# Feed-forward networks from seven products: a new order of splits, root and spread, and weight sums made by DMA

## The reference

```
def rms_norm(x, g):
    y = x * rsqrt(mean(x * x, axis=-1) + 1e-6)
    return y * g
def swiglu(h, w_gate, w_up, w_down):          # 1024 -> 2816 -> 1024
    return (silu(h @ w_gate) * (h @ w_up)) @ w_down
h = h + 0.5 * swiglu(rms_norm(h, gain), w_gate, w_up, w_down)
```

## Time and profile before

| | |
|---|---|
| median of 3 runs | 2536.75 us (2528.5 to 2537.78) |
| the profiled execution's own time | 2528.84 us |
| its span, first to last instruction | 2526.6 us |
| TensorE busy | 2434.3 us, 96% |
| VectorE busy | 1708.9 us, 68% |
| ScalarE busy | 1078.2 us, 43% |
| GpSimd busy | 97.3 us, 4% |
| mean granted TensorE clock | 0.986 of full speed |
| DMA | 213.00 MB, 84 GB/s; SP's queue takes 25.7% of the 16 engines' time |

### The profile page before, as it was taken

How to read it: one execution, slowest core, us unless ns; L and a number is a source line. 1 busy time by engine, 2 the same in 40 slices (tenths; PEclk the granted TensorE clock), 3 DMA queues, 4 the chain that set the end, 5 groups by cost and what they waited for, 6 DMA issues and landing times.

```text
span 2526.6 us, 48964 instructions
## 1 busy us (share of the span) xinstructions
PE 2434.3 (96%) x20418; PEld 2245.1 (89%) x20418; DVE 1708.9 (68%) x2926; ACT 1078.2 (43%) x1959; POOL 97.3 (4%) x107
## 2 busy tenths in 40 slices
PE   7999999998999999999999999999989999999998
PEld 6999999996877989888999999898877888989896
DVE  6877775646656879678878675242976445879684
ACT  5444343334434535346535343112874234535352
POOL 0000001000320000001000002000000000000001
PEclk9999999999999999999999999999999999999999
DMA  3323232220001233232223232232212333233332
GB/s 132 99 88 125 76 114 90 76 84 4 4 12 49 100 98 108 93 108 67 94 91 125 77 101 95 77 92 75 55 46 75 96 92 100 76 101 101 100 108 68
DMA packets 72378, 213.00 MB, mean 84 GB/s; under 512 B 12796, under 2 KB 20028, under 8 KB 72032
## 3 DMA queue, kind: packets, MB, share of 16 engines
q1 hardware_dynamic: 70496, 209.03, 25.7%
q0 software_dynamic: 480, 0.73, 0.1%
q10 hardware_dynamic: 1184, 0.12, 0.0%
HBM read 207.61 MB, written 2.20 MB: 83 GB/s over the span
## 4 chain that ended last, share of the span: by engine, by line
PE 75%; DVE 12%; ACT 5%; issue 5%; DMA 2%; DVEq 0%; ACTq 0%
PE PS L851 20%; PE PS L1374 20%; PE PS L1331 7%; PE PS L1333 7%; PE PS L1332 7%; DVE WL L936 4%; ACT WH L924 2%; DMA WR<-in_ffn_up 2%; PE PS L1680 1%; PE PS L1681 1%; PE PS L1679 1%; DVE SUMS L962 1%; PE PS L2230 1%; DVE P L2862 1%; PE PS L2799 1%
## 5 line engine op out<-in xcount | busy, mean ns | idle before, releaser
L1331 PE MATMUL PS<-OPH,WH 128*128 128x256 f32 (+1 forms) x2112 | 603.7, 286 | 17.7 <-DMA CST<-in_consts 15.7
L1333 PE MATMUL PS<-OPH,WL 128*128 128x256 f32 (+1 forms) x2112 | 602.1, 285 | 0.0
L1332 PE MATMUL PS<-OPL,WH 128*128 128x256 f32 (+1 forms) x2112 | 600.2, 284 | 0.0
L924 ACT ACTIVATE WH<-WR 128x1024 fp32r<-128x1024 f32 (+2 forms) x305 | 304.6, 1000 | 608.8 <-PE PS L851 274.1
L936 DVE TENSOR_TENSOR WL<-WR,WH 128x1024 fp32r<-128x1024 f32 (+2 forms) x305 | 352.7, 1158 | 195.2 <-ACT WH L924 194.8
L1331 PEld LDWEIGHTS PS<-OPH,WH 128*128 128x128 f32 x2112 | 403.2, 191 | 18.8 <-issue 15.7
L1332 PEld LDWEIGHTS PS<-OPL,WH 128*128 128x128 f32 x2112 | 403.4, 191 | 0.3
L1333 PEld LDWEIGHTS PS<-OPH,WL 128*128 128x128 f32 x2112 | 402.6, 191 | 0.0
L924 ACT ACTIVATE WH<-SUMS 128x512 fp32r<-128x512 f32 x352 | 210.9, 623 | 259.6 <-DVE SUMS L962 213.4
L936 DVE TENSOR_TENSOR WL<-SUMS,WH 128x512 fp32r<-128x512 f32 x352 | 234.4, 686 | 29.3 <-ACT WH L924 28.9
L851 PE MATMUL PS<-NHI,WH 128*128 128x264 f32 (+2 forms) x960 | 235.3, 310 | 1.5 <-ACT TMP L2597 1.0
(11 more groups left out here) (462 smaller groups left out, 4593.0 us busy)
## 6 DMA issues: line engine op xcount, KB each, us to landing
WR<-in_ffn_gate SPq DMA_DIRECT2D x88, 512.0 KB, 3.7
WR<-in_ffn_up SPq DMA_DIRECT2D x88, 512.0 KB, 3.7
WR<-in_ffn_down SPq DMA_DIRECT2D x64, 512.0 KB, 4.3
WR<-in_ffn_down SPq DMA_DIRECT2D x32, 384.0 KB, 3.4
WR<-in_w_gate SPq DMA_DIRECT2D x24, 512.0 KB, 3.6
WR<-in_w_out SPq DMA_DIRECT2D x16, 512.0 KB, 3.6
WR<-in_in_rkv SPq DMA_DIRECT2D x12, 512.0 KB, 3.5
WR<-in_w_branch SPq DMA_DIRECT2D x24, 256.0 KB, 2.6
```

What stands on the lines that cost most here:

```text
L924: e.activation(split_unit(i)[0][:, 0:w], src, ACT.Copy).then_inc(S["w_hi"], 1)
L1331: e.matmul(o, wh[:, at:at + 128], hi, start=k == 0 and s in (1, 2, 5), stop=False, skip_group_check=True)
L1332: e.matmul(o, wh[:, at:at + 128], lo, start=False, stop=False, skip_group_check=True)
L1333: last = e.matmul(o, wl[:, at:at + 128], hi, start=False, stop=k == 3, skip_group_check=True)
```

## The change

The order of the steps changes in two places. "root" stands before (0, 6), "spread" behind (0, 7); on VectorE the reciprocal is taken in step (0, 6), before the splits that the step frees. At the end of an FFN the item of the first down product stands before f(21). In w_out all splits are taken one step earlier.

Of the four sums of units 1 to 21, those of e and c are no longer made by VectorE. GpSimd issues, per unit, two DMAs that copy 256 KB each from DRAM (block 0 and block 3), waits for them, and issues one DMA that adds block 2 to both. Units take turns between two places, SUMS and SUMS_ODD; the latter lies over T2F, so unit 1 waits for the low part of T3. Unit n waits for the splits of e and c of unit n-2, and for sum 2 of the unit before. The splits of c and e, and VectorE's sum 2, wait for the third DMA (`sum1`).

```diff
-    steps = [("p", 0, 1), ("p", 0, 5), ("p", 0, 2), ("p", 0, 6), ("root", 0, 0)]
+    steps = [("p", 0, 1), ("p", 0, 5), ("p", 0, 2), ("root", 0, 0), ("p", 0, 6)]
     for n in range(1, FT):
-        steps += [("p", n, 1), ("p", n, 2)]
+        steps += [("p", n, 1), ("p", n, 2), ("p", n - 1, 7)]
         if n == 1:
             steps.append(("spread", 0, 0))
-        steps += [("p", n - 1, 7), ("p", n, 5), ("p", n - 1, 3), ("p", n, 6), ("p", n - 1, 4)]
+        steps += [("p", n, 5), ("p", n - 1, 3), ("p", n, 6), ("p", n - 1, 4)]
...
-    return ring + [[("e", f, FT - 1), ("g", f, FT - 1)], [("f", f, FT - 1)]] + downs(2)
+    last = downs(2)
+    return ring + [[("e", f, FT - 1), ("g", f, FT - 1)]] + last[:1] + [[("f", f, FT - 1)]] + last[1:]
...
+def sums_before(f, n):
+    return f * (2 * FT + 1) + (2 * n + 1 if n else 0)
...
+        SUMS_ODD, _ = place("SUMS_ODD", at - 8 * HALF, 2, 512)
         SUMS, at = place("SUMS", at, 4, 512)
...
-                q.wait_ge("summed", 3 * (FT * f + n) + made)
-                return SUMS[:, at, :]
+                if made > 1 or n == 0:
+                    q.wait_ge("summed", sums_before(f, n) + made - (1 if n else 0))
+                else:
+                    q.wait_ge("sum1", 16 * ((FT - 1) * f + n))
+                return first_sums(n)[:, at, :] if made == 1 else SUMS[:, at, :]
...
-            if (f, n, which) in sums_made:
+            if (f, n, which) in sums_made or which == 1 and n > 0:
                 return
...
+            if f:
+                q.wait_ge("w_lo", U["f", f - 1, FT - 1] + 1)
             q.wait_ge("neg", f + 1)
...
+        def pool_first_sums(e, q, f):
+            for n in range(1, FT):
+                turn = (FT - 1) * f + n
+                name, j = FFN[f][1:3][n % 2], 2 * (n // 2)
+                if n > 1:
+                    q.wait_ge("w_lo", U["e", f, n - 2] + 1)
+                    q.wait_ge("w_lo", U["c", f, n - 2] + 1)
+                    q.wait_ge("summed", sums_before(f, n - 1) - 1)
+                else:
+                    q.wait_ge("t3_lo", t3_made(f, 3))
+                    q.wait_ge("t4f", 4 * f + 4)
+                into = first_sums(n)
+                e.dma_start(into[:, 0, :], dram[name][j][:, 0:512]).then_inc(S["sum_in"], 16)
+                e.dma_start(into[:, 1, :], dram[name][j + 1][:, 512:1024]).then_inc(S["sum_in"], 16)
+                q.wait_ge("sum_in", 32 * turn)
+                e.dma_start(into, dram[name][j + 1][:, 0:512].unsqueeze(1).broadcast_to([128, 2, 512]),
+                            accum_op=ALU.add).then_inc(S["sum1"], 16)
...
                 if kind == "p" and y == 6:
                     if x == 0:
                         dve_late_operands(e, q, f, 2)
+                        if f == 2:
+                            dve_two_roots(e, q)
+                        else:
+                            dve_root(e, q, s, R)
...
-                if name != "w_out" or m > 0:
+                if name != "w_out":
                     act_split(e, q, U[name, m] + 2)
-                if m == DT - 1:
+                if name == "w_out" or m == DT - 1:
                     act_split(e, q, U[name, m] + 3)
...
+            pool_first_sums(e, q, 0)
             pool_squares(e, q, 1, FULL)
...
+            pool_first_sums(e, q, 1)
             pool_to_meta(e, q)
+            pool_first_sums(e, q, 2)
             pool_squares(e, q, 5, FULL)
             pool_project_2(e, q)
             pool_squares(e, q, 6, REAL, 4)
+            pool_first_sums(e, q, 3)
             pool_squares(e, q, 7, REAL, DT - 1)
```

More of the change, by code:

```diff
@@ L171, in ffn_ring, with t3_made @@
             ring.append([("ab", f, n + 2)])
-    return ring + [[("e", f, FT - 1), ("g", f, FT - 1)], [("f", f, FT - 1)]] + downs(2)
+    last = downs(2)
+    return ring + [[("e", f, FT - 1), ("g", f, FT - 1)]] + last[:1] + [[("f", f, FT - 1)]] + last[1:]
+def sums_before(f, n):
+    return f * (2 * FT + 1) + (2 * n + 1 if n else 0)
+def t3_made(f, i):
+    return 1 if f == 0 else 4 * f - 3 + i + 1
 class Weights:
@@ L256, in order_loads @@
                 ended = self.done["p", f, max(n - 1, 0), 6]
-                load(("raw", f, n, 0), dram[name][j], a, ended, ("summed", 3 * (FT * f + n) + 3))
+                load(("raw", f, n, 0), dram[name][j], a, ended, ("summed", sums_before(f, n + 1)))
                 ended = self.freed[self.at["f", f, n]] + 0.5
@@ L271 @@
 SEMAPHORES = (
-    ["load", "cst", "eps", "small", "gate_up", "rows", "stored", "summed", "neg", "g12", "t1f", "t2f", "t3f", "t4f", "t_hi", "t_lo", "t3_hi", "t3_lo", "t4_hi", "t4_lo", "rsq",
+    ["load", "cst", "eps", "small", "gate_up", "rows", "stored", "summed", "neg", "g12", "t1f", "t2f", "t3f", "t4f", "t_hi", "t_lo", "t3_hi", "t3_lo", "t4_hi", "t4_lo", "rsq", "sum_in", "sum1",
      "r1", "r2", "r5", "c11", "c12", "c22", "e0", "e1", "d_t"]
@@ L940, in dve_split, with first_sums @@
                     dve_sum(e, q, *W.items[i][1:], 3)
+        def first_sums(n):
+            return SUMS_ODD if n % 2 else SUMS[:, 0:2, :]
         sums_made = set()
         def dve_sum(e, q, f, n, which):
-            if (f, n, which) in sums_made:
+            if (f, n, which) in sums_made or which == 1 and n > 0:
                 return
             sums_made.add((f, n, which))
-            raw, b = raw_blocks(f, n), FT * f + n
+            raw, b, done = raw_blocks(f, n), FT * f + n, sums_before(f, n) - (1 if n else 0)
             before = (f, n - 1) if n else (f - 1, FT - 1)
@@ L964, in dve_sum @@
             if which == 2:
-                q.wait_ge("summed", 3 * b + 1)
-                e.tensor_tensor(SUMS[:, 2, :], SUMS[:, 1, :], raw[:, 0, :], ALU.add).then_inc(S["summed"], 1)
+                if n:
+                    q.wait_ge("sum1", 16 * ((FT - 1) * f + n))
+                else:
+                    q.wait_ge("summed", done + 1)
+                e.tensor_tensor(SUMS[:, 2, :], first_sums(n)[:, 1, :], raw[:, 0, :], ALU.add).then_inc(S["summed"], 1)
             if which == 3:
-                q.wait_ge("summed", 3 * b + 2)
+                q.wait_ge("summed", done + 2)
                 e.tensor_tensor(SUMS[:, 3, :], SUMS[:, 2, :], raw[:, 1, :], ALU.add).then_inc(S["summed"], 1)
@@ L1022, in dve_negative @@
             e.tensor_scalar(NEGS[:, f, :], gains, -1.0, None, ALU.mult).then_inc(S["neg"], 1)
-        def t3_made(f, i):
-            return 1 if f == 0 else 4 * f - 3 + i + 1
         def act_operands(e, q, f, k, square):
@@ L1252, in pe_sums_after, with dve_folded_sums @@
                     pe_square_sums(e, q, f, TMP, k)
-        def dve_two_roots(e, q):
+        def dve_folded_sums(e, q):
             q.wait_ge("rsum", 5)
@@ L1260, in dve_two_roots @@
                                    op1=ALU.add).then_inc(S["folded"], 1)
+        def dve_two_roots(e, q):
             q.wait_ge("root", 4)
@@ L1570, in dve_ffn @@
                 if kind == "root" and f == 2:
-                    dve_two_roots(e, q)
-                elif kind == "root":
-                    dve_root(e, q, s, R)
+                    dve_folded_sums(e, q)
                 if kind == "part" and y == 1:
```

## The result

The changed kernel took 2587.17 us (median of 4 runs, 2579.01 to 2596.73) against 2535.44 us for the kernel before (median of 4, 2528.5 to 2537.78): a ratio of 1.021, 95% interval 1.0162 to 1.0258. The prediction of 2534 us and its range up to 2580 were wrong. The interval of the ratio is about 12 us wide to either side, so differences against the changed kernel are known no better than that.

The account below looks back on a forecast made before the run. TensorE, busy 96% of the span, was taken to bound the kernel. The terms -13.0 - 4.5 - 3.9 - 9.0 + 22.8 + 5 gave -2.6 us, so 2534 us; the whole range was 2508 to 2580.

Parts of the forecast that it names:

- D: Sums by DMA: time from a chain's trigger to its landed sum, put at 9.6 us, between 6.8 and 14.5.
- End of an FFN: First down products: four split waits go, -13.0 us, and the half clock behind them, -4.5 us.
- w_out: Fourth block's split wait: 2.5 of 3.6 us go, plus half of the half clock's 2.8 us: -3.9 us.
- Root and spread: Start of each FFN: moving reciprocal and spread would alone remove the spread's waits for the reciprocal, 7.7 us.
- The chain's size: GpSimd's DMAs per unit: both copies 3.7 us, the accumulating DMA taken as two passes, 5.9 us.
- The starts: Unit 1 of each FFN: chain delays group (0, 7) and spread, +22.8 us; half clock after idling, +5 us.
- The steady unit: Units of an FFN: the chain fits, ScalarE's wait before c goes, and up to 12.4 us nothing is later.
- -9.0: Last group of a unit: TensorE's 14 waits for c22 go as VectorE is relieved, 9.0 us gained.
- The contention: DMA engines shared with SP's two loads of a unit: up to 2.2 us more on the chain.
- rival B: Split of c in every unit: chain sets the period from 12.4 us; at 13, +40 us, 2577 us; chance 0.23.
- C: End of an FFN: first down product waits for banks or load instead; +15 us, 2552 us; chance 0.07.
- A: Starts of the FFNs: accumulating costs what a copy does, chain 7 us; -18 us, 2519 us; chance 0.30.

Follow-up runs that it names:

- e9: The kernel before with only the order at the end of each FFN changed, all sums on VectorE: 2511.5 us, ratio 0.992.
- e10: The kernel before with only w_out's splits taken one step earlier, all sums on VectorE: 2532.2 us, ratio 1.0004.
- e11: The kernel before with only the root, reciprocal and spread moved, all sums on VectorE: 2528.3 us, ratio 0.9983.
- e4: The changed kernel with unit 1's first two sums made by VectorE, the DMA chain beginning with unit 2: 2551.1 us, ratio 1.0086.
- e1: The changed kernel with its new order only: all four weight sums on VectorE, no sums by DMA: 2509.2 us, ratio 0.9918.
- e6: e4 with a third buffer for the first sums, so that a chain is issued one unit earlier: 2520.0 us, ratio 0.9963.
- e7: The changed kernel with the accumulating DMA aimed at an unread buffer, readers waiting for the copies alone; sums incomplete: 2521.1 us, ratio 0.9966.
- e3: The changed kernel without the accumulating DMAs, only the two copies; two of four sums lack a summand: 2495.7 us, ratio 0.9866.
- e12: e6 with only e's sum by DMA (one 256 KB copy, one 256 KB accumulate), c's by VectorE: 2498.7 us, ratio 0.987.
- e2: e1 plus the change's three DMAs per unit into a buffer nobody reads, VectorE making all sums: 2582.0 us, ratio 1.0204.

## Why the prediction was wrong

The working asked the right question (does the chain D fit between two uses of a buffer?), had its undisturbed length right, and then answered with that length where the chain is disturbed, and with a rest of the unit that it took to stay as it was.

- *End of an FFN, -17.5.* Right: e9 measured -20 (-26 to -15).
- *w_out, -3.9.* Its 2.5 us of shorter wait are there (3.6 to 1.1). The step that failed is that nothing came in their place: the prediction did not name what is late next. It is the first group of FFN 1, 2.8 us, with the low clock around it, and the net is nothing (e10). An equal wait stands in the changed kernel.
- *Root and spread.* "Alone this would take away the 7.7 us" held for the waits and about half for the time (e11: 1 to 8 us). The three parts together were priced at -29 and gave -21.
- *The chain's size.* Copies 3.7 and accumulate 5.9, D = 9.6; measured 4.2 and 5.83, 10.0 at the start of FFN 1. The Trainium skill, Collectives: The Full Stack, Part 3, says that the add's two source reads halve the rate, which gave the same 5.9 us; the trace agrees, with 3.1 us of all engines against 1.4 for a plain copy. The Trainium skill, SBUF — State Buffer, Who interferes with whom, has VectorE holding up GpSimd's descriptors, and exempts tensor_tensor. Nothing here speaks for such a hold-up: 160 of the 168 copies' issues took 0.54 to 0.70 us, and in the eight of 1.1 us VectorE ran nothing.
- *The starts, +22.8 and +5.* Right in sum. TensorE waits 4.2 + 7.4 + 9.9 + 9.0 = 30.5 us; less the 7.7 of spreads set off, 22.8. It came out unevenly, not 6 to 7 us each; the prediction's own terms (delay of the group, spread, old wait) give 6.8, 6.9, 8.7 and 8.1, so "6 to 7" was a misreading of its sum for FFN 2 and 3. Against an order that was to gain 7.7 at the spreads, 22.8 + 5 + 7.7 = 35.5; taking the chain out of the start gave back 31 to 36 us (e4), 35 by the trace.
- *The steady unit: "with 9.6 even that wait would go, and up to 12.4 nothing is later than today".* This is the step that failed. The units were costed at nothing and credited with -9.0; they cost 42 us against e1. ScalarE's wait before c did not go. In the 52 units from 3 on that have no down products near, it fell from 2.6 to 1.8 us in the mean, and the split of c(k+2) came 12.4 us after e(k), as before the change, because the chain took 11.75 us and not 9.6. And the part behind it, from the split of c to the end of e, which the prediction kept at 8.3 us, grew from 8.5 to 9.8: sum 2 waits for the landing too, and sometimes for SP's slower loads, and ScalarE waits for sum 2 (54.2 us in place of 3.3). Two units so took 22.2 us in place of 20.9. The threshold of 12.4 us was therefore too high: it held only with the old 8.3 us. That rest of the unit is not a fixed cost by itself (10.8 us in e6 and 11.0 in e7, where c is split 2.4 us earlier and two units take 20.9); the late landing and the longer rest cost the time together. The -9.0 was right where nobody waits for the third DMA: e3 has no such wait among its largest.
- *The contention* was set at "up to 2.2 more" and used only for the range. It acts twice: two landings in a row each stretch (7.6 and 8.9 us in the unit shown), and SP's loads stretch from 3.7 to 5.1 and 5.6. The prediction had a clue: its own upper end for D, 14.5 us, lay above its own threshold, and rival B was nevertheless given 0.23.
- *The rivals.* B was nearest. Its mechanism, waiting for the chain, is most of the loss in the units: 31 of 42 us went with an earlier chain (e4 against e6), 41 of 45 between units 0 and 21 with nobody waiting (the change against e7). But it asked for a steady D above 12.4, with the 8.3 us fixed, so its price, two units of 21.3 us, was too low, and its sign came true by half: units of 11.1 us, but an accumulate of 6.0 us in the median, over 8 in 16 of 84. C did not happen; A's short accumulate did not either.

In the sum: order -21, units +42, starts +31 (all from ratios) make +52, and 2.1% of 2530 us is 53. This is no second proof: the three are steps between the same four ratios.

What stays open: how the 41 us of e7 divide between ScalarE's own wait for the landing and sum 2's; how the 24 us between e6 and e12 divide between the halved traffic and the place of the sum; e12's order without w_out's earlier splits, which by e10's rows should be no worse, was not tried.

## What to carry to other kernels

Price a new chain of DMAs by what it takes among the transfers that are in flight where it will run, not by one that runs alone. Before comparing it with the time that it is given, list everything that will wait for its landing: here a second reader, sum 2, made the rest of the unit longer, and with it the allowed time shorter. Loads that are issued only when their buffer comes free have little slack to lend: most of what another queue took from them was paid by their first reader (e2), and it matters who that is (e6). When work moves to DMAs, give the chain a buffer more and as few accumulated bytes as will do: against the same order without DMA sums (e1), this idea cost 74 us, 11 with a third buffer and a start by VectorE, and gained 12 when one sum of the two was left to VectorE as well.

## What was not expected of the hardware

An accumulating DMA of 512 KB held GpSimd 1.24 us for its issue, where a copy of 256 KB took 0.57, and it occupied the 16 DMA engines 3.1 us against 1.4 us for a plain one. At a mean share of 40% (24.5 and 15.3) these engines were far from full, and still landings beside them grew by a third to a half: SP's 512 KB loads from 3.7 to 5.1 and 5.6 us. The copies alone, 5.4% of the engines' span in e3, slowed nothing (3.8 and 3.7 us).
